# Rotary embedding of two-head query and key tiles: the exchange of halves moved from a TensorE permutation to transfers within SBUF

## The reference

```python
def apply_rope(x, cos, sin):
    x1, x2 = jnp.split(x, 2, axis=-1)
    c = cos[None, :, None, :]
    s = sin[None, :, None, :]
    return jnp.concatenate([x1 * c - x2 * s, x1 * s + x2 * c], axis=-1)

def global_gqa(...):      # mixer A: 8 query heads, 2 key heads, all keys
    q = apply_rope(rmsnorm(heads(q, N_HEADS_A), qn), cos, sin) * scale
    k = apply_rope(rmsnorm(heads(k, N_KV_A), kn), cos, sin)
    ...                   # softmax(q k^T) v, context queries and keys without rope

def window_gqa(...):      # mixer C: 8 query heads, 2 key heads, window of +-128 keys
    q = (apply_rope(heads(q, N_HEADS_C), cos, sin) * scale)...
    k = apply_rope(heads(k, N_KV_C), cos, sin)

def neighbourhood_attn(...):  # mixer B: 8 heads, no rope
```

## Time and profile before

| | us |
|---|---|
| median of three runs | 3213.38 |
| the profiled execution | 3217.06 |
| its span | 3215.2 |
| PE busy | 2985.7 (93%) |
| DVE busy | 1230.4 (38%) |
| ACT busy | 780.8 (24%) |
| mean granted TensorE clock | 0.986 |

### The profile page before, as it was taken

One profiled execution on the slowest core, in us unless ns is written; L12 is line 12 of the kernel. 1 busy time (PEld: TensorE's weight loads), 2 busy tenths in 40 slices (PEclk: granted clock), 3 DMA queues, 4 the chain that ended last, 5 costly groups with the idle time before them and its releaser, 6 DMA issues.

```text
span 3215.2 us, 34266 instructions
## 1 busy us (share of the span) xinstructions
PE 2985.7 (93%) x13594; PEld 1557.3 (48%) x13594; DVE 1230.4 (38%) x2367; ACT 780.8 (24%) x1358; POOL 81.6 (3%) x156
## 2 busy tenths in 40 slices
PE   7999999989999999999999889999999998999998
PEld 3556556555555556544544444444444434444433
DVE  1454564773034465761475623111111533111112
ACT  3233444331122353331252002000002122000001
POOL 0000000000000000000000000000000000000000
PEclk9999999999999999999999899999999999999999
DMA  6222221223113232342111025999996224999996
GB/s 266 81 72 71 77 94 51 90 81 105 66 56 131 85 112 96 121 151 92 44 53 40 0 104 197 409 410 410 409 410 249 79 79 166 409 410 410 410 410 266
DMA packets 139661, 584.24 MB, mean 182 GB/s; under 512 B 10176, under 2 KB 10176, under 8 KB 127520
## 3 DMA queue, kind: packets, MB, share of 16 engines
q1 hardware_dynamic: 118848, 502.56, 39.9%
q0 software_dynamic: 20704, 80.16, 7.5%
HBM read 580.58 MB, written 2.10 MB: 181 GB/s over the span
## 4 chain that ended last, share of the span: by engine, by line
PE 79%; DVE 8%; ACT 6%; DMA 4%; issue 2%; SPq 0%; ACTq 0%; DVEq 0%
PE BIG L711 43%; PE PJ L711 20%; PE BIG L1307 4%; DMA W<-in_exp_w 3%; PE PJ L965 3%; PE PT L944 3%; PE BIG L927 2%; PE BIG L931 1%; ACT ARENA L1457 1%; DVE SPILL L1709 1%; ACT ARENA L1447 1%; DVE STAT L1845 1%; ACT ARENA L1645 1%; PE PJ L760 0%; DMA W<-in_units 0%
## 5 line engine op out<-in xcount | busy, mean ns | idle before, releaser
L711 PE MATMUL PJ<-HT,W 128*128 128x512 f32 (+1 forms) x1792 | 647.1, 515 | 22.6 <-ACT ARENA L1429 11.0
L711 PE MATMUL BIG<-ARENA 128*64 128x512 f32 (+1 forms) x2688 | 476.6, 460 | 2.5 <-DVE ARENA L2120 2.5
L711 PEld LDWEIGHTS PJ<-HT,W 128*128 128x128 f32 x1792 | 337.0, 193 | 278.6 <-issue 240.1
L711 PE MATMUL BIG<-W,ARENA 128*64 128x512 f32 (+1 forms) x1664 | 370.9, 579 | 35.9 <-ACT ARENA L1645 18.5
L711 PEld LDWEIGHTS BIG<-ARENA 128*64 128x64 f32 (+1 forms) x2688 | 246.4, 163 | 225.2 <-issue 225.2
L711 PE MATMUL BIG<-HT,W 128*128 128x512 f32 (+1 forms) x768 | 322.8, 581 | 5.5 <-DVE CONST L1891 3.6
L711 PE MATMUL BIG<-ARENA,W 128*128 128x512 f32 (+1 forms) x832 | 317.2, 543 | 1.5 <-ACT ARENA L1601 1.5
L1457 ACT ACTIVATE ARENA<-PT 128x512 f32<-128x512 f32 (+1 forms) x280 | 150.1, 572 | 470.2 <-PE PT L944 469.0
L711 PEld LDWEIGHTS BIG<-W,ARENA 128*64 128x64 f32 (+1 forms) x1664 | 143.1, 142 | 248.7 <-issue 210.0
L2147 DVE SCALAR_TENSOR_TENSOR XC<-BIG,MOD,XC 128x512 f32<-128x512 f32 x128 | 90.2, 747 | 417.6 <-PE BIG L1307 417.6
L711 PEld LDWEIGHTS BIG<-ARENA,W 128*128 128x128 f32 x832 | 157.8, 190 | 159.2 <-issue 153.6
(11 more groups left out here) (238 smaller groups left out, 2082.0 us busy)
## 6 DMA issues: line engine op xcount, KB each, us to landing
W<-in_exp_w SPq DMA_DIRECT2D x192, 1024.0 KB, 15.4
ARENA<-in_exp_w SPq DMA_DIRECT2D x192, 1024.0 KB, 17.5
W<-in_units SPq DMA_DIRECT2D x89, 1024.0 KB, 4.9
W<-in_mod_rows POOLq DMA_DIRECT2D x128, 512.0 KB, 3.7
ARENA<-in_bias_b POOLq DMA_DIRECT2D x16, 448.0 KB, 5.2
XC<-in_x SPq DMA_DIRECT2D x1, 3072.0 KB, 10.1
W<-in_mod_vectors POOLq DMA_DIRECT2D x2, 1024.0 KB, 6.8
out_t<-HT SPq DMA_DIRECT2D x8, 256.0 KB, 2.2
```

The lines of the kernel that those rows point to most:

```text
L711: ins = pe.matmul(out, lhsT, rhs, start=start, stop=stop)
```

## The change

The permutation leaves TensorE. ACT issues four transfers within SBUF per rope, each moving 32 partitions of 512 fp32 columns (64 KB) from the tile to ROPE_T with neighbouring blocks of 32 partitions exchanged. The sign that was in `rot` moves into the sine table. The item of the order is split into `shift_*` (the transfers) and `rope_*` (DVE's three operations). ACT waits, ahead of the transfers, for the normed or copied tile, and for the rope before, since ROPE_T is one buffer. For the pairs of A, `norm_q` comes right behind the projection of q; `shift_q` stands in the middle of the gates and `rope_q` behind them, for the C pairs of layer 0 too, where it stood in the middle.

```diff
-        return out + [("rope_k", i)] + through("g", parts) + [("rope_q", i)]
+        gates = through("g", parts)
+        return out + [("shift_k", i)] + gates[:KT // 2] + [("rope_k", i), ("shift_q", i)] + gates[KT // 2:] + [("rope_q", i)]
     gates = through("g", parts)
     out = through("q", parts)
-    if kind == "C":
-        return out + gates[:KT] + [("rope_q", i)] + gates[KT:] if parts == 2 else out + gates + [("rope_q", i)]
-    if parts == 2:
-        return out + gates[:KT] + [("norm_q", i)] + gates[KT:] + [("rope_q", i)]
-    return out + [("norm_q", i)] + gates + [("rope_q", i)]
+    half = len(gates) // 2
+    if kind == "A":
+        out.append(("norm_q", i))
+    return out + gates[:half] + [("shift_q", i)] + gates[half:] + [("rope_q", i)]
...
-    return {..., "norm_q": 3, "rope_k": 2, "rope_q": 2}[what]
+    return {..., "norm_q": 3, "rope_k": 1, "rope_q": 1, "shift_k": 0, "shift_q": 0}[what]
...  PE
                     elif what.startswith("rope_"):
                         if PAIRS[x][0] == "A":
-                            pe.wait_ge(qk_normed, me.next("qk_normed"))
-                        else:
-                            raw = raw_use[what[5:], x]
-                            pe.wait_ge(pj_free[raw[0]], raw[1] + 1)
-                        src = K[:, kv % 2, 0:N] if what == "rope_k" else Q[:, x % 2, 0:N]
-                        use = next_pj()
-                        pe.matmul(PJ[use[0]][:, 0:N], const("rot"), src, start=True, stop=True)\
-                            .then_inc(pj_filled, 1)
+                            me.next("qk_normed")
...  ACT
+                    elif what.startswith("shift_"):
+                        which = what[6:]
+                        src = K[:, kv % 2, 0:N] if which == "k" else Q[:, x % 2, 0:N]
+                        if PAIRS[x][0] == "A":
+                            act.wait_ge(qk_normed, normed[which, x])
                         else:
-                            me.next("qk_normed")
-                    elif what.startswith("rope_"):
-                        me.next_pj()
+                            raw = raw_use[which, x]
+                            act.wait_ge(pj_free[raw[0]], raw[1] + 1)
+                        if me.next("shifts") > 1:
+                            act.wait_ge(qk_roped, me.seen["shifts"] - 1)
+                        for block in range(4):
+                            other = block ^ 1
+                            act.dma_start(ROPE_T[32 * block:32 * block + 32, :], src[32 * other:32 * other + 32, :])\
+                                .then_inc(qk_shifted, 16)
...  DVE
-                        use = me.next_pj()
-                        dve.wait_ge(pj_filled, use[2])
-                        roped = me.next("qk_roped") - 1
-                        if roped:
-                            dve.wait_ge(qk_roped, roped)
-                        dve.tensor_tensor(ROPE_T, PJ[use[0]][:, 0:N], const("sin"), ALU.mult)\
-                            .then_inc(pj_free[use[0]], 1)
+                        shifts = me.next("qk_roped")
+                        dve.wait_ge(qk_shifted, 64 * shifts)
+                        dve.tensor_tensor(ROPE_T, ROPE_T, const("sin"), ALU.mult)
                         link(dve.tensor_tensor(dst, dst, const("cos"), ALU.mult))
-                        dve.wait_ge(pj_free[use[0]], use[1] + 1)
                         dve.tensor_tensor(dst, dst, ROPE_T, ALU.add).then_inc(qk_roped, 1)
...  constants
-    packed[:, COFF["sin"]:COFF["sin"] + N] = np.tile(np.sin(ang).T, (4, 1))
+    packed[:, COFF["sin"]:COFF["sin"] + N] = np.concatenate([-np.sin(ang).T, np.sin(ang).T] * 2, axis=0)
```

More of the change, by code:

```diff
@@ L55 @@
     _at += _n
-CONSTS = [("ident", P), ("blk", P), ("ones", P), ("rot", P), ("cos", N), ("sin", N),
+CONSTS = [("ident", P), ("blk", P), ("ones", P), ("cos", N), ("sin", N),
           ("mprev", P), ("mnext", P), ("sel", 2), ("sel16", N_EXPERTS)]
@@ L130, in weight @@
         return 2 if item[3] == 0 else 1
-    return {"vt": 0.5, "v_tokens": 2.5, "norm_k": 3, "norm_q": 3, "rope_k": 2, "rope_q": 2}[what]
+    return {"vt": 0.5, "v_tokens": 2.5, "norm_k": 3, "norm_q": 3, "rope_k": 1, "rope_q": 1, "shift_k": 0, "shift_q": 0}[what]
 def schedule(layer):
@@ L146, in schedule @@
             done += weight(item)
-            if item[0].startswith(("norm_", "rope_")):
+            if item[0].startswith(("norm_", "shift_", "rope_")):
                 least = min(at + (before is not None and before >= at), tiles - 1)
@@ L464, in build @@
         qk_roped = sem("qk_roped")
+        qk_shifted = sem("qk_shifted")
         gate_tanh = sem("gate_tanh")
@@ L1385, in attention @@
                 waiting = None
+                raw_use, normed = {}, {}
                 for item in order:
@@ L1398, in attention @@
                         n = NA if which in ("k", "v") else nq
+                        raw_use[which, i] = use
                         act.wait_ge(pj_filled, use[2])
@@ L1433, in attention @@
                         act.activation(SQT[:, 0:n], SQT[:, 0:n], ACT.Exp, scale=-0.5).then_inc(qk_rs, 1)
+                        normed[what[5:], x] = me.next("qk_normed")
                         if what == "norm_k":
-                            act.wait_ge(qk_normed, me.next("qk_normed"))
+                            act.wait_ge(qk_normed, normed["k", x])
                             square(waiting)
-                        else:
-                            me.next("qk_normed")
-                    elif what.startswith("rope_"):
-                        me.next_pj()
+                    elif what.startswith("shift_"):
[3 more added lines that the diff above has]
+                            act.wait_ge(qk_normed, normed[which, x])
+                        else:
+                            raw = raw_use[which, x]
[6 more added lines that the diff above has]
+                                .then_inc(qk_shifted, 16)
                     elif what == "E":
@@ L2195, in constants @@
     packed[:, COFF["ones"]:COFF["ones"] + P] = 1
-    half = HD // 2
     for b in range(2):
@@ L2199, in constants @@
         packed[b * HD:(b + 1) * HD, a:a + HD] = 1
-        for m in range(half):
-            packed[b * HD + m + half, COFF["rot"] + b * HD + m] = -1
-            packed[b * HD + m, COFF["rot"] + b * HD + m + half] = 1
     t = np.arange(N)
```

## The result

| | before | after |
|---|---|---|
| median of the runs in the same call, us | 3212.96 (3211.86 to 3215.34) | 3253.39 (3251.15 to 3256.59) |
| the profiled execution, us | 3217.06 | 3256.59 |
| its span, us | 3215.2 | 3254.2 |

The ratio is 1.0122, 95% interval 1.0109 to 1.0136: 40 us slower. The forecast was 3223, its range ended at 3241. The direction was as written and the forecast change a quarter of the real one; of the mechanism one part, ACT's held queue, had been priced at nothing.

The account below looks back on a forecast made before the run. The prediction took the ACT and DVE chain through the rope to bound 13 of 20 ropes, not PE. Terms of +3.9 us and +5.5 for the clock gave +9.4 on 3217.06, 3226.5; as a median 3223 us, range 3207 to 3241.

Parts of the forecast that it names:

- What bounds the kernel: At 13 of 20 ropes PE's first scores wait for the rope, 10.9 us in total; the ACT and DVE chain decides there.
- Rival 2: PE sets the end after all: 20 permutations and half the bank waits go, -20 us, 3193; chance 0.05.
- the 0 of the prediction: At the 13 ropes ending a pair's preparation, removing the permutation is worth 0, at most 13 x 1.1 = 14 us.
- The issue and the landing of the transfers: Per rope: four issues hold ACT's queue 1.3 us, the last landing 3.1 us after the first began; ends 1.7 and 6.5.
- Where that sits in ACT's order: Layer 1, transfers between exponentials and tanh: +1.0 us each ahead of A1 to A3, +0.8 together for C1 to C3.
- The clock: Longer idle pieces ahead of the scores let 5 more of 16 transitions fall to half pace, 1.1 us each: +5.5 us.
- its upper end: Clock falls at all 16 transitions, each halving PE's pace for 3.4 us with nothing to absorb it: 27 us.
- The order of norm_q and of the rope behind SG: Layer 0, norm_q earlier and rope behind all gates: A1, A2 +1.15 us each, A3 -2.0, C1 to C3 +1.2 each.
- k's chain in layer 1: A0 and C0: gates end sooner, but two landings in sequence eat the PE time; -0.2 us and -1.5 us.
- Rival 3: Landing takes 4.9 us in place of 2.1 through another transfer in flight: +49 at most, 3250 in its middle; chance 0.11.
- What would show it: Signs: PE's busy time some 20 us less, its rope wait 35 us or more over 16 places, layer 0 C1 to C3 waiting.

Follow-up runs that it names:

- b1_no_permutation: Kernel before with the permutation and its bank left out and nothing in its place, halves not exchanged: 3211.29 us, ratio 0.9994.
- i2_sp_early: Changed kernel with transfers issued by SP, two buffers for them, and for all 20 ropes transfers and rope moved earlier in the order: 3187.51 us, ratio 0.9921.
- j1_permutation_early: Kernel before, permutation still on TensorE, with ropes moved ahead of gates where a group of eight matmuls ends, k's rope between the values: 3207.70 us, ratio 0.9977.
- i1_sp_issue: Changed kernel with the same transfers at the same places of the order, issued by SP's queue in place of ACT's: 3224.96 us, ratio 1.0034.
- a3_one_transfer: Changed kernel with one transfer of 128 partitions (256 KB) per rope in place of four of 64 KB, halves not exchanged: 3227.68 us, ratio 1.0043.
- g1_issue_only: Changed kernel without the halves' exchange; ACT still issues four transfers per rope, into an unread buffer, and DVE doesn't wait: 3239.96 us, +16.2 over no transfers.
- a2_fillers: Changed kernel with 1 to 7 dummy matmuls on PE behind the last O ahead of each A and C pair: 3252.69 us, ratio 1.0125.
- both filler kernels: a2_fillers, and the changed kernel with its dummy matmuls cut to end before the rope does: 3252.69 and 3245.97 us.
- a4_order_only: Kernel before with only the new order of norm_q and rope_q, the permutation staying on TensorE: 3219.16 us, ratio 1.0015.

## Why the prediction was wrong in size

**What bounds the kernel: right.** Rival 2 (PE sets the end, -20 us) fell with b1_no_permutation: -2 us. That run takes out all 20 permutations and not the 13 alone, but its profile tells them apart: the nine pairs that end at A1 to A3 of both layers and at C1 to C3 of layer 1, all with their one rope at such a place, came out 3.1 us longer together, and the seven others 15.8 shorter (in a fast execution; the medians don't show so much). So at the 13 places the permutation was worth the 0 of the prediction. What the prediction left out is that about the same 20 us can be had once the rope is off the chain, as i2_sp_early and j1_permutation_early together show.

**The step that failed: "The issue and the landing of the transfers", with "Where that sits in ACT's order".** The nearest row was read for the wrong property. SP's 0.33 us was taken since ACT's queue "needs no software either", but the price goes with the transfer: for 32 partitions within SBUF 0.61 us on ACT's queue and 0.59 on SP's, 2.4 to 2.9 us for four on ACT where 1.3 was forecast, the last landing 4.3 us after the first issue ahead of A2 (1229.66 to 1233.99) where 3.1 was. The landing itself, 2.1 us, was right in the median. The sum gave this term +3.8 us in layer 1 and named the tanh, delayed by 0.2, as hidden. In fact i1_sp_issue, which takes these issues out of ACT's queue, removes 28 of the 40 us; a3_one_transfer, with a quarter of the issues, 26. Both parts of the mechanism are shown: ACT's held queue, with the tanh in it (g1_issue_only, +16.2), and the landing that DVE awaits (+13.4).

**The clock: mis-sized.** The prediction let 5 of 16 transitions fall, at 1.1 us. Measured were falls at 12 of 16, where the kernel before has none, and some of them lasted 6.8 us and not 3.4. The half-pace time grew by 61 us (20 to 82), as much as 18 stretches of the 3.4 us of the earlier trace rows, more than the 16 of its upper end. Where fillers covered the wait without outlasting it, a pair gained 1.5 to 1.7 us and not 1.1. Over the twelve pairs other than those that end at A0 and C0, a2_fillers is 17 us shorter than the kernel after in the profiles; the medians of both filler kernels show 0.7 (with the overrun of 12.6 in it) and 7.4. So the clock's share lies somewhere from 1 to 17 us by these runs, against a forecast of 5.5, and stays open; fillers add work of their own, and the runs scatter.

**The terms one by one**, from scores to scores, the kernel after less the kernel before, where the measured column holds both chain and clock (A0 is counted from the start of the span in layer 0, and from C3's scores of layer 0 in layer 1):

| pair that ends at | forecast without clock | measured |
|---|---|---|
| layer 0: A0, C0 | -1.1, -1.0 | -0.8, +3.5 |
| layer 0: A1, A2, A3 | +1.15, +1.15, -2.0 | +0.3, +2.9, +4.2 |
| layer 0: C1, C2, C3 | +1.2 each | +4.9, +3.8, +5.7 |
| layer 1: A0, C0 | -0.2, -1.5 | -0.4, +1.1 |
| layer 1: A1, A2, A3 | +1.0 each | +2.0, +2.3, +2.7 |
| layer 1: C1, C2, C3 | +0.3 each | +3.5, +1.6, +0.2 |

They sum to some +37 (the forecast's to +3.9; its clock term, +5.5, is not among them). Ahead of A1 to A3 of layer 1 the chain was close: +0.7 for +1.0 at A2; the rest of the 2.3 is the clock's, as the fillers gave back 1.7 there. The order of norm_q and of the rope behind SG cost less than forecast where it was tested alone (a4_order_only, with the permutation still there: A1 and A2 +1.5 together for +2.3, A3 -2.9 for -2.0, C1 to C3 +1.7 together for +3.6), so it isn't what was missing. What went wrong in layer 0, beside the clock, was the transfers between the exponentials and the gate's tanh. The kernel after, ahead of A3:
```profile
508.54 1.91 ACT L1476 ACTIVATE W<-W 128x2048 f32<-128x2048 f32 x1
...
512.31 0.52 ACTq L1446 DMA_DIRECT2D ARENA<-ARENA  x1
...
514.80 0.38 ACT L1398 ACTIVATE ARENA<-PJ 128x256 f32<-128x256 f32 x1 [1.53 <-issue]
...
518.25 1.23 PE L921 MATMUL BIG<-ARENA 64*128 64x512 f32 x2 [4.92 <-DVE ARENA L1786]
```
The gates were done at 509.12 + 3.62 = 512.74; the tanh came 2.1 us later, since ACT was at the issues, and those stood behind the Silu. The prediction had this ("with the shifts' issues behind the Silu some of it is given back") and gave it no price: it took -2.0 where its rows had -1.75. Ahead of C1, still of the kernel after:
```profile
630.73 3.72 PE L712 MATMUL PJ<-HT,W 128*128 128x256 f32 x16 [0.56 <-DVE ARENA L1808]
...
635.74 0.69 DVE L1784 TENSOR_TENSOR ARENA<-ARENA,CONST 128x512 f32<-128x512 f32 x1 [0.41 <-DMA ARENA<-ARENA]
...
637.82 0.70 PE L921 MATMUL BIG<-ARENA 64*128 64x256 f32 x4 [2.77 <-DVE ARENA L1786]
```
A pair that had no wait at its scores now has 2.77 us, as predicted in kind (2.4), and the landing ends it, not SG.

**k's chain in layer 1**: -0.4 for -0.2 at A0, but not by the chain that was forecast. In the kernel after:
```profile
1148.08 9.25 ACTq L1446 DMA_DIRECT2D ARENA<-ARENA  x5
...
1152.79 0.69 DVE L1784 TENSOR_TENSOR ARENA<-ARENA,CONST 128x512 f32<-128x512 f32 x1 [3.90 <-DMA ARENA<-ARENA]
...
1157.38 0.60 ACT L1398 ACTIVATE ARENA<-PJ 128x512 f32<-128x512 f32 x1 [9.28 <-issue]
...
1160.89 2.08 PE L921 MATMUL BIG<-ARENA 64*128 64x512 f32 x4 [7.23 <-DVE ARENA L1786]
```
The first row groups the last issue for k with the four for q. k's first issue was at 1146.26, a unit of 1 MB went out on SP's queue at 1146.57, and k's last transfer landed at 1152.69: 6.4 us where the forecast had 2.8 (1126.6 to 1129.4; its own sum for issues and landing was 3.1). q's four issues then waited in ACT's queue for k's rope, and the tanh, whose gates were done at 1152.40, stood behind them until 1157.38. So PE idles 7.23 us where "5 us and more" was written. Rival 3 (slow landing, 0.11) held where a load was issued at about the same time, up to 5.6 us, but the median stayed 2.1: its mechanism was partly there, its price for all 16 chains was not. That its sum of 3250 came nearest was luck in the main. By the Trainium skill's page "DMA: Bandwidth & Descriptors" ("Queues, rings and completion order"), each DMA engine takes turns between its queues packet by packet. By that one would expect a meeting to cost a small transfer little; these meetings show up to 5.6 us against 2.1. If the load is the cause, which was not tried by itself, the traces do not agree, and the measurement decides.

**What would show it**: PE's wait of 35 us or more over 16 places came (51.3, 16), and so did the wait at the scores of C1 to C3 of layer 0 (2.6 to 2.8 us). PE's busy time some 20 us less did not: the clock took it back and 8 us more.

## What to carry to other kernels

Price a new transfer by a row of the same shape and endpoints, count its issues as work of the engine that makes them, and then ask which instruction stands behind them in that queue: here four issues for each rope, behind the exponentials and ahead of a tanh, cost 28 us more over the 20 ropes than on a queue that was free, where they cost almost nothing. Work taken from the busiest engine beside a longer chain turns into waiting (b1_no_permutation: 17 us less work, 19 us more wait for the rope, and 2 us won), and where the chain grows too, as in the kernel after, the clock can take back more than the work that was removed. Move the chain's start ahead, then the work that was taken away counts (i2_sp_early, 0.9921 [0.9907, 0.9934]).

## What the runs showed of the hardware

- The issue of a transfer within SBUF of 32 partitions by 512 fp32 took 0.51 us (the first of four) to 0.61 on ACT's queue and 0.51 to 0.59 on SP's (medians 0.61 and 0.59, at times 1.4 and 2.1); one of 128 partitions by 512 took 0.47 on ACT's (a3_one_transfer); a load of 1 MB from HBM took 0.33 on SP's. The difference by kind of transfer was not expected. Four of 64 KB took 2.4 us to issue; one of 256 KB for each rope cost 3.9 us in the whole kernel where four cost 30.
- 64 KB within SBUF landed 2.1 us after the issue in the median. At the 7 ropes of 20 in the kernel after whose transfers had no load in flight beside them, all landed in 1.9 to 2.1 us. At 7 ropes some took over 3 us, up to 5.6, and at each of these a load of 512 KB or 1 MB was issued within 1.1 us of one of the four issues (the four ropes of k among them, with loads of 1 MB at 337.11, 576.84, 1146.57 and 1322.28). That the load is the cause was not tried by itself.
- Behind the idle pieces ahead of the scores, 1.6 to 7.2 us, PE's clock was lower at 12 of 16 transitions (two passes took 1.22 us that took 0.70), and other matmuls became 29.7 us dearer in total. The length of the piece does not tell where: behind 1.64 us (A0 of layer 0) the clock was 0.50, behind 2.08, 2.33, 2.63 and 2.83 us (C2 of layer 1, A1 and C3 of layer 0, A3 of layer 1) it was 1.00.
